# Closing an eight-pass expert stage with tokens on partitions instead of features on partitions

## The reference, cut to what matters

```
def _moe_swiglu(h, w_router, b_router, w_exp_in, w_exp_out):
    logits = (h @ w_router) + b_router
    top_val, top_idx = lax.top_k(logits, 2)
    top_w = jax.nn.softmax(top_val, axis=-1)
    combine = sum(one_hot(top_idx, 8) * top_w[..., None], axis=-2)
    out = zeros_like(h)
    for e in range(8):
        out = out + combine[..., e:e + 1] * _swiglu(h, w_exp_in[e], w_exp_out[e])
    return out

    x = x + gate_f * f              # gate_f: one row of 1024 for the prompt, one for the sample
y = _rmsnorm(x, p["g_final"])       # x * rsqrt(mean(x*x) + 1e-6) * g_final, over the features
```

## Time and profile before

| What | us |
|---|---|
| Median of 3 runs | 1502.15 (1499.78 to 1505.53) |
| Profiled execution, its own time | 1501.98 |
| Span of its profile | 1500.2 |
| PE busy | 1403.1 (94%) |
| DVE busy | 1022.5 (68%) |
| ACT busy | 785.6 (52%) |

### The profile page before, as it was taken

One profiled execution on the slowest core, in us unless ns is written; L12 is line 12 of the kernel. 1 busy time (PEld: TensorE's weight loads), 2 busy tenths in 40 slices (PEclk: granted clock), 3 DMA queues, 4 the chain that ended last, 5 costly groups with the idle time before them and its releaser, 6 DMA issues.

```text
span 1500.2 us, 24401 instructions
## 1 busy us (share of the span) xinstructions
PE 1403.1 (94%) x9312; PEld 1234.5 (82%) x9312; DVE 1022.5 (68%) x1417; ACT 785.6 (52%) x1062; POOL 38.2 (3%) x66
## 2 busy tenths in 40 slices
PE   5899999998889999998999999988899999999984
PEld 4788999875889999996989988767588888888863
DVE  2376999874554444334769987744788898889855
ACT  2534448634433333225443586243778788778852
POOL 0000100000000000000001000000200000000100
PEclk8999999999989999999999999999899999999996
DMA  9856743124446867434858661245689999999951
GB/s 310 228 169 197 235 141 125 59 85 154 135 140 201 255 217 237 177 100 121 246 159 290 198 186 57 85 140 188 223 320 386 383 387 388 378 386 385 384 203 68
DMA packets 280099, 327.33 MB, mean 218 GB/s; under 512 B 32319, under 2 KB 190471, under 8 KB 280007
## 3 DMA queue, kind: packets, MB, share of 16 engines
q1 hardware_dynamic: 273042, 314.29, 63.0%
q10 hardware_dynamic: 5492, 6.53, 1.3%
q0 software_dynamic: 1472, 5.24, 1.0%
HBM read 310.84 MB, written 15.17 MB: 217 GB/s over the span
## 4 chain that ended last, share of the span: by engine, by line
PE 88%; DVE 5%; ACT 2%; DMA 2%; SPq 1%; issue 1%; ACTq 0%; POOLq 0%; POOL 0%; DVEq 0%
PE mmp L819 14%; PE mmp L821 14%; PE mmp L820 13%; PE mmp L1221 8%; PE mmp L1223 8%; PE mmp L1222 8%; PE mmp L813 7%; PE py L789 2%; PE px L869 2%; PE py L885 1%; PE lg L985 1%; PE lg L869 1%; PE px L1027 1%; DVE hT L1796 1%; DMA ring<-in_w_ada_dram 1%
## 5 line engine op out<-in xcount | busy, mean ns | idle before, releaser
L819 PE MATMUL mmp<-hT_hi,wm_hi 128*128 128x320 f32 (+1 forms) x976 | 308.3, 316 | 13.1 <-DVE merged_lo L2023 5.1
L821 PE MATMUL mmp<-hT_hi,ring_lo 128*128 128x320 f32 (+1 forms) x976 | 306.2, 314 | 0.0
L820 PE MATMUL mmp<-hT_lo,wm_hi 128*128 128x320 f32 (+1 forms) x848 | 263.3, 310 | 0.0
L1827 DVE TENSOR_TENSOR ring_lo<-ring,wm_hi 128x1024 fp32r<-128x1024 f32 (+1 forms) x124 | 148.1, 1201 | 86.5 <-ACT wm_hi L1423 84.3
L819 PEld LDWEIGHTS mmp<-hT_hi,wm_hi 128*128 128x128 f32 (+1 forms) x976 | 184.7, 189 | 18.6 <-issue 8.4
L821 PEld LDWEIGHTS mmp<-hT_hi,ring_lo 128*128 128x128 f32 (+1 forms) x976 | 184.3, 189 | 0.2
L1423 ACT CAST wm_hi<-ring 128x1024 fp32r<-128x1024 f32 (+1 forms) x124 | 126.7, 1029 | 101.5 <-PE mmp L821 80.7
L820 PEld LDWEIGHTS mmp<-hT_lo,wm_hi 128*128 128x128 f32 (+1 forms) x848 | 159.3, 188 | 0.2
L1380 ACT ACTIVATE tmp<-mmp 128x320 f32<-128x320 f32 x70 | 30.7, 438 | 231.5 <-PE mmp L821 163.1
L1915 DVE SCALAR_TENSOR_TENSOR conv<-u_conf,dwc,conv 128x350 f32<-128x350 f32 x240 | 132.2, 581 | 3.1
L2048 DVE TENSOR_TENSOR wd_lo<-ring,wd_hi 128x2048 fp32r<-128x2048 f32 (+1 forms) x34 | 75.7, 2229 | 64.6 <-ACT wd_hi L1587 64.5
(11 more groups left out here) (371 smaller groups left out, 2866.2 us busy)
## 6 DMA issues: line engine op xcount, KB each, us to landing
ring<-in_w_in_dram SPq DMA_DIRECT2D x104, 512.0 KB, 4.6
ring<-in_w_exp_in_dram SPq DMA_DIRECT2D x64, 512.0 KB, 8.2
more<-in_w_exp_in_dram SPq DMA_DIRECT2D x64, 512.0 KB, 11.2
ring<-in_w_ada_dram SPq DMA_DIRECT2D x56, 512.0 KB, 7.2
more<-in_w_exp_out_dram SPq DMA_DIRECT2D x48, 512.0 KB, 6.9
ring<-in_w_ffn_in_dram SPq DMA_DIRECT2D x44, 512.0 KB, 5.9
wide<-in_w_ada_dram SPq DMA_DIRECT2D x40, 512.0 KB, 7.6
ring<-in_w_branch_dram SPq DMA_DIRECT2D x48, 256.0 KB, 2.8
```

The source lines that it names most:

```text
L819: nc.tensor.matmul(out, w_hi, x_hi, start=is_first, stop=False)
L820: nc.tensor.matmul(out, w_hi, x_lo, start=False, stop=False)
L821: return nc.tensor.matmul(out, w_lo, x_hi, start=False, stop=is_last)
L1827: V.tensor_tensor(mix_rows(ring_lo, l, s, r), mix_rows(ring, l, s, r), mix_hi(l, s, r).bitcast(F32), ALU.subtract).then_inc(mix_lo_ready, 1)
```

## The change

The late rows are gathered before the last pass has ended. What they hold of the last pass's rows is stale, and gets weight zero. The last pass's own y is not stored: for each token that has a row in it, a selection matrix `Sz` [128 tokens, 128 rows] holds the token's weight at that row (DVE, L2270 of the new file); PE transposes it to `SzT` (L1286), ACT copies it (L1720). After the last pass DVE multiplies y by the gate, once for the prompt's gate row and once for the sample's. For each third t of the tokens PE then forms, in two banks, `SzT`'s product with that gated y (L1315, 512 columns wide) plus the transposed residual, by products of `xT` with the identity (L1318, eight of 128 columns). DVE adds the other rows (`both_rows`, with gate; `add_z`), and ACT gets the sum of squares of a token along its row. The root and reciprocal are of one number a token. The gate rows and g_final must now lie along the free dimension on every partition: sixteen DMAs in the mixer of layer 1 store the gate by 4-byte elements to `gate_dram`, and SP loads it back broadcast behind the last weights. SP issues the outputs.

```diff
@@ SP, layer 1, gates
                         if l:
                             clear_rows(j)
+                        if l and j == 8:
+                            sp.wait_ge(mods_added, DEPTH * ADA_PAIRS)
+                            for s_ in range(2):
+                                for c in range(DC):
+                                    sp.dma_start(gate_dram[s_, c * P:(c + 1) * P].unsqueeze(1),
+                                                 mods[:, l, 40 + c, s_:s_ + 1]).then_inc(gate_stored, 16)
@@ SP, behind the last pass's loads
+                    sp.wait_ge(xg_done, last + 1)
+                    sp.wait_ge(gate_stored, 16 * 2 * DC)
+                    sp.dma_start(gate_rows[0][:], gate_dram[0:1, :].broadcast_to([P, D])).then_inc(gate_loaded, 16)
+                    sp.dma_start(gate_rows[1], gate_dram[1:2, :].broadcast_to([P, D])).then_inc(gate_s_loaded, 16)
+                    sp.dma_start(fin_row, g_final.unsqueeze(0).broadcast_to([P, D])).then_inc(fin_loaded, 16)
+                    for t in range(3):
+                        sp.wait_ge(out_ready, t + 1)
...
@@ POOL
                 if c == 1:
-                    pool.wait_ge(y_saved, last * 16 + 16)
-                    nc.gpsimd.sem_inc(y_free, 1)
+                    pool.wait_ge(chunk_done, last * CPP + (ring_no["moe", 1, 0] + 12))
@@ PE, in the last pass, then behind it
+                                    if k == 10 and is_last_pass:
+                                        pe.wait_ge(sz_ready, 1)
+                                        for t in range(3):
+                                            ins = nc.tensor.transpose(lg[:, t * P:t * P + rows[t]], Sz[0:rows[t], t, :],
+                                                                      ident[0:rows[t], 0:rows[t]])
+                                        ins.then_inc(sz_tr, 1)
-                    pe.wait_ge(y_evac, last + 2)
+                    pe.wait_ge(szT_ready, 1)
                     for t in range(3):
-                        pe.wait_ge(rows_summed, t + 1)
-                        for c in range(DC):
-                            ins = nc.tensor.transpose(sum_bank(c)[:, t * P:t * P + rows[t]],
-                                                      y_late[0:rows[t], t, c * P:(c + 1) * P],
-                                                      ident[0:rows[t], 0:rows[t]])
...
-            norm_sums(4)
-            pe.wait_ge(h_ready, DC * 5)
...
+                        for h in range(2):
+                            pe.wait_ge(y_gated_ready, h + 1 if t < 2 else 3)
+                            c = slice(h * 512, (h + 1) * 512)
+                            nc.tensor.matmul(z_banks(t)[0:rows[t], c], SzT[:, t * P:t * P + rows[t]],
+                                             y_gated[t // 2][:, c], start=True, stop=False)
+                            for c in range(4 * h, 4 * h + 4):
+                                ins = nc.tensor.matmul(z_banks(t)[0:rows[t], c * P:(c + 1) * P],
+                                                       xT[:, c, t * P:t * P + rows[t]], ident[:], start=False,
+                                                       stop=(c % 4 == 3))
+                        ins.then_inc(z_done, 1)
@@ ACT, in the last pass, then behind it
+                            if k == 11 and is_last:
+                                act.wait_ge(sz_tr, 1)
+                                copy(SzT[:], lg[:, 0:T]).then_inc(szT_ready, 1)
+                            if k == 15 and is_last:
+                                act.wait_ge(ab_ready, 1)
+                                act.wait_ge(early_rows, 16 * 3)
+                                for t in range(3):
+                                    m = P if t < 2 else TS
+                                    nc.scalar.activation(x_tok[0:m, t, :], x_tok[0:m, t, :], ACT.Copy,
+                                                         scale=w_ab[0:m, 0, t:t + 1]).then_inc(early_scaled, 1)
+                                nc.scalar.activation(root[:, 0, :], eps[:, 0:1], ACT.Sqrt)
-                            if k == CPP - 1:
+                            if k == CPP - 1 and not is_last:
...
+                        act.wait_ge(z_added, t + 1)
+                        nc.scalar.activation(z_banks(t)[0:m, :], y_late[0:m, t, :], ACT.Square,
+                                             accum_out=sum_sq[0:m, t, :]).then_inc(z_squared, 1)
+                        act.wait_ge(z_squared, t + 1)
+                        nc.scalar.activation(root[0:m, t, :], sum_sq[0:m, t, :], ACT.Sqrt, scale=1.0 / D,
+                                             bias=eps[0:m, 0:1]).then_inc(root_ready, 1)
@@ DVE, router, then last pass
+                    link(V.tensor_scalar(row_end, cum[:, NE - 1:NE], NE - 1.0, float(P), ALU.add, ALU.mult))
...
+                    link(V.tensor_scalar(row_z, pos_ab[:, 1, :].unsqueeze(2), row_end, None, ALU.subtract))
+                    link(V.tensor_scalar(in_z, row_z, -0.5, None, ALU.is_gt))
+                    link(V.tensor_tensor(w_z, in_z, w_ab[:, 1, :].unsqueeze(2), ALU.mult))
+                    link(V.tensor_tensor(w_ab[:, 1, :].unsqueeze(2), w_ab[:, 1, :].unsqueeze(2), w_z, ALU.subtract))
...
+                            if k == 5 and is_last:
+                                dve.wait_ge(y_saved, last * 16)
+                                for t in range(3):
+                                    ins = V.tensor_scalar(Sz[:, t, :], iota_f[:], row_z[:, t, :], w_z[:, t, :],
+                                                          ALU.is_equal, ALU.mult)
```

More of the change, by code:

```diff
@@ L319, in build @@
         gap, w_top, w_ab, swap, row_0 = table(3), table(2, 3), table(2, 3), table(2, 3), table(3, 1)
+        row_z, in_z, w_z, row_end = table(3, 1), table(3, 1), table(3, 1), table(1)
+        sum_sq, root, r_root = table(3, 1), table(3, 1), table(3, 1)
+        assert table_at[0] <= 480
+        Sz = y[:, 0:3 * P].rearrange("p (t s) -> p t s", t=3)
+        SzT = std
+        y_gated = (y, hid_tok[:, 0:D])
+        fin_row = more[:, 0, D:2 * D]
+        gate_rows = (xrow, more[:, 1, D:2 * D])
+        gate_dram = nc.dram_tensor("gate_dram", (2, D), F32).ap()
         rlT = std[0:NE, :]
@@ L1259, in run_pass @@
                                 hid_transposes(2)
-                            if k == 16 and not is_last:
+                            if k == 16 and not is_last_pass:
                                 pe.wait_ge(xrow_full, p * 16 + 16)
@@ L2228, in _, with both_rows @@
                     run_pass(last, True)
[L2229 to L2230 removed]
+                    def both_rows(t):
                         m = P if t < 2 else TS
                         dve.wait_ge(early_scaled, t + 1)
[L2233 to L2240 removed]
@@ L2242, in _ @@
-            norm(4)
-            for b in range(6):
-                t, g = b // 2, b % 2
-                m = P if t < 2 else TS
-                dve.wait_ge(y_tr, b + 1)
-                V.tensor_copy(x_tok[0:m, t, g * 512:(g + 1) * 512], mmp[0:m, b % 4, :]).then_inc(y_copied, 1)
+                        link(V.scalar_tensor_tensor(y_late[0:m, t, :], y_late[0:m, t, :], w_ab[0:m, 1, t:t + 1],
+                                                    x_tok[0:m, t, :], ALU.mult, ALU.add))
+                        link(V.tensor_tensor(y_late[0:m, t, :], y_late[0:m, t, :], gate_rows[t // 2][0:m, :], ALU.mult))
@@ new lines, in add_z, with end_row @@
+                    def add_z(t):
+                        m = P if t < 2 else TS
+                        dve.wait_ge(z_done, t + 1)
+                        V.tensor_tensor(y_late[0:m, t, :], z_banks(t)[0:m, :], y_late[0:m, t, :],
+                                        ALU.add).then_inc(z_added, 1)
+                    def end_row(t):
+                        m = P if t < 2 else TS
+                        dve.wait_ge(root_ready, t + 1)
+                        link(V.reciprocal(r_root[0:m, t, :], root[0:m, t, :]))
+                        V.scalar_tensor_tensor(x_tok[0:m, t, :], y_late[0:m, t, :], r_root[0:m, t, :], fin_row[0:m, :],
+                                               ALU.mult, ALU.mult).then_inc(out_ready, 1)
@@ new lines, in _ @@
+                    dve.wait_ge(late_rows, 16 * 3)
+                    dve.wait_ge(gate_loaded, 16)
+                    for t in range(2):
+                        both_rows(t)
+                    dve.wait_ge(chunk_done, last * CPP + (n0 + CPP))
+                    dve.wait_ge(gate_s_loaded, 16)
+                    for h in range(2):
+                        c = slice(h * 512, (h + 1) * 512)
+                        V.tensor_tensor(y_gated[0][:, c], mmp[:, 2 + h, :], gate_rows[0][:, c],
+                                        ALU.mult).then_inc(y_gated_ready, 1)
@@ L2251 @@
+                    V.tensor_tensor(y_gated[1], mmp[:, 2:4, :].rearrange("p a b -> p (a b)"), gate_rows[1],
+                                    ALU.mult).then_inc(y_gated_ready, 1)
+                    both_rows(2)
```

(7 more changed lines are left out.)

68 lines of the change are left out of this document (26 added, 42 removed).

## The result

The changed kernel takes 1491.78 us (median of 5 runs, 1489.74 to 1493.42) where the kernel before takes 1502.15 (1499.78 to 1505.53): ratio 0.9927, 95% interval 0.9911 to 0.9944. In a later comparison on another occasion it was 1489.53 against 1503.26, ratio 0.9911 [0.9896, 0.9927]. The gain is 10 to 14 us; I had forecast 23.5 and a time of 1478.6.

What follows compares the result with a forecast made beforehand. The end was taken as bound by latency: 44.6 us in series after the last matmul. Replacing them by 21.2 gains 23.4, ending at 1476.8; with 1.8 us of execution beyond the span, 1478.6, range 1475 to 1487.

Steps and rivals of the forecast that it cites:

- the 21.3 that my sum has behind the last matmul's start: Tail: the new series of DVE, PE, ACT and output DMA takes 21.2 us from the last matmul's end, replacing 44.6.
- the arrival of the late rows: End of the last pass: late gather asked for near 1440, landed between 1449.2 and 1451.9, DVE starting at 1451.3.
- The gate stores: Layer 1's mixer: sixteen stores in SP's queue delay the j=9 load 1.2 us, with some 20 us to spare; cost nothing.
- The 7.3 us for the packets' time: Gate stores in layer 1's mixer: 2048 packets at 57 ns each over 16 engines take 7.3 us, hidden.
- Rival C: Layer 1's mixer: gate stores run serially; at 4.2 us each the stall is 39.7 us, time 1518; chance 3%.
- the bound of 1454: Behind the last pass: latest start of DVE's `both_rows` on the late rows, taken at 1451.3 with bounds 1450.6 and 1454.
- rival B: End of the last pass: late rows or gate row come after 1454, or last weights are delayed; 1481 to 1484.5; 10%.
- rival A: PE's pause after the last pass: clock falls to half speed, losing 2.8 to 3.3 us: 1482, worst near 1489.5; 15%.
- DVE's own four operations: Behind the last pass: DVE's operations for two thirds of the late rows take 5.2 us with links, until 1456.5.
- A third of PE's products: Tail: two 512-column selection products and eight identity products take 3.6 us at the full clock, 7.2 at half.
- rival D: End: something else, such as output DMAs or ACT-DVE hand-overs at twice the price, gives 1483 to 1484; 9%.
- DVE's small router operations and the selection: Router and passes: five tiny operations 1.0 us, three selection operations in waits; costed nothing, at most 1 us each.

Runs made afterwards that it cites:

- b_stores: The kernel before with the sixteen gate stores alone added in SP's queue at the same place: 1502.47 us, ratio 1.0002.
- a_spread: The changed kernel with one gate store behind each of the sixteen branch and out loads of layer 1: 1492.75 us, ratio 0.9937.
- b_small480: The kernel before with table `small` 480 columns wide instead of 448, later tiles 128 bytes further on: six passes 288.36 us for 286.79 (one execution).
- a_best2: The changed kernel with gates transposed and stored by two DMAs, `small` at 448, late broadcasts, PE's operands first, one DVE wait moved: 1478.43 us, ratio 0.9840.
- b_small512: The kernel before with table `small` 512 columns wide, later tiles 256 bytes further on: six passes 286.79 us, as before (one execution).
- a_bcast_late: The changed kernel with the sample's gate row and g_final broadcasts asked for later, at the last pass's chunk before the last: 1487.42 us (one execution).
- a_filler: The changed kernel with six unused identity products on PE right behind the last pass: first bank 1.82 us for 3.43, tail 24.06 (one execution).
- a_flat_stores: The changed kernel with each gate store replaced by one of 128 adjacent zeros, 16 packets for 2048: 1486.59 us, ratio 0.9908.
- a_reorder: The changed kernel with DVE making PE's gated operands after only the first both_rows, the others later: 1483.20 us, ratio 0.9860.
- a_pool_stores: The changed kernel with the sixteen gate stores issued from POOL's own queue, earlier, instead of SP's: 1493.08 us, ratio 0.9948.

## Why the prediction was wrong

The forecast of 1478.6 was 14.8 us below the first profiled run of the changed kernel, 1493.42. By the table these are: start of the span 2.7 (noise), mixer 3.9, router -0.4, first pass 2.8, six passes 1.6, last pass 0.5 more than my 0.33, tail 3.7 more than the 21.3 that my sum has behind the last matmul's start.

Only part of it repeats. The second profile, 5.9 us above the forecast, has 4.1 in the tail, 1.6 in the six passes, 0.5 in the last one, 3.0 in the first, nothing in the mixer, the router 0.6 shorter and a start 2.6 earlier. So the step that failed in both, and by most, is the arrival of the late rows with the pause and the clock behind it. The stores, costed at nothing, are 2.6 us in the mean of seven profiles. The place of the tiles was no term of the sum, and the first pass stays open.

**The gate stores were costed at nothing.** I had the load of j=9 leave 1.2 us late, land in 5 us and have some 20 us to spare. All three were wrong in the changed kernel. First, SP's issues were not 0.55 us each as in the earlier trace rows, they were 0.72 (11.58 for sixteen), and the load left 4.0 us late. Second, it took 12.5 us to land for 5.4: in 884 to 892 us DMA was 0.63 to 0.66 busy at 31 to 53 GB/s, where before 876 to 888 ran at 152 to 241.

```profile
884.00:888.00 4.00, 4.00 (x31) 3.31 (x30) 3.68 (x8) 3.97 (x7) 0.00 (x0) 1.00 0.63 31
888.00:892.00 4.00, 4.00 (x29) 4.00 (x29) 3.69 (x6) 3.04 (x8) 0.00 (x0) 1.00 0.66 53
892.00:896.00 4.00, 4.00 (x33) 3.48 (x31) 1.35 (x3) 1.07 (x3) 0.00 (x0) 1.00 1.05 364
```

Third, I read the spare time from PE, 20 us until it takes up the chunk. The chunk is read first by ACT's cast and DVE's subtraction. Before the change the load had landed at 881.1 and ACT cast the chunk at 889.35, 8.2 us later. The 4.0 and the 7.1 us used that up and left the 2.9 that ACT waited (the chunk's cast before, then in the changed kernel):

```profile
889.35 1.04 ACT L1423 CAST wm_hi<-ring 128x1024 fp32r<-128x1024 f32 x1
```

```profile
895.08 1.04 ACT L1456 CAST wm_hi<-ring 128x1024 fp32r<-128x1024 f32 x1 [2.93 <-DMA ring<-in_w_in_dram]
```

The 7.3 us for the packets' time look nearly right, since q1's packets took 63.5% of b_stores's span, 954.3 us, for 63.0% or 945.1 before. That is luck. In the trace's record of single packets a 4-byte one takes 9 ns and not my 57, about 1.3 us in all over 16 engines. The time went into the weights' own 1 KB packets: in 884 to 892 us of the changed kernel most of them took 46 ns as ever, but a few up to 4.2 us, 253 ns in the mean, where before 876 to 888 has 56. Rival C had the right place and the right sign of the effect, with a wrong mechanism: the stores are not serial at 4.2 us, they slow what shares the engines with them. The page of the Trainium skill that I weighed and set aside, "DMA: Bandwidth & Descriptors" (section "Specifications"), says that a transfer below 512 B becomes a read-modify-write. I had taken that as double time for the small packets; their recorded 9 ns don't show it. In a_spread too the sixteen stores raised the DMA share of 30 us from 0.27 to 0.74 by longer weight packets (124 ns in the mean for 51). Whether a read-modify-write is behind that, no run shows.

**The tiles' place was no step of the sum.** `small` grew by 32 columns, and the prediction read the line as bookkeeping. It costs 1.6 us in six passes, found by b_small480 and taken back in a_best2. In the last pass b_small480 has 58.78 us for 57.98, as much as the changed kernel with its three transposes (0.42 us, 0.33 predicted), but b_small512 has 58.45, so that there the placement is not all.

**The late rows came 2.1 us later than I took them.** They were asked for at 1451.38, against my 1440 plus the 11.4 us by which the pass ends later: as said. DVE took them up at 1464.77 for 1451.3 plus 11.4, which is 1.5 us beyond my upper estimate of their arrival too, though inside the bound of 1454 that I had set for DVE's start. POOL's three issues had 3.2 us between first and last, for 3.65 in the earlier trace rows. But I let them land at 5.3 to 7.9 us and they took 9.4. I had the rows go first and the 1.5 MB of broadcast rows behind them. SP issued the broadcasts 3.7 us before the gather was even asked for, so that they and the last weights were in the engines when it came (share 1.03 to 1.05 until 1460):

```profile
1447.68 0.35 SPq L743 DMA_DIRECT2D xrow<-gate_dram  x1
1448.08 0.42 SPq L744 DMA_DIRECT2D more<-gate_dram  x1
1448.55 0.43 SPq L745 DMA_DIRECT2D more<-in_g_final_dram  x1
```

I had said that "the new 2.8 MB have some 6 us before 1451.3", at 0.80 share; 2.8 MB at the 385 GB/s of the passes alone are 7.3. a_bcast_late took 1 MB away and DVE's wait was gone. This is rival B in cause, below its own condition of 1454, and rival A in consequence, which I had priced apart: with DVE's own four operations (5.2 us, as predicted) PE paused 4 us instead of 1.3, and the clock was at half speed for its first bank, 1.7 us by a_filler. Together the 2.1 and the 1.7 us are about the tail's 3.7. My figure for A was 2.8 to 3.3; two variants come to it, a_flat_stores and a_spread, where the clock was at 0.50 before PE's first product and PE's products to the end took 21.8 us instead of 19.0. a_reorder cut the pause to 1.75 us and kept the full clock, with late rows that came no earlier.

**What was right.** A third of PE's products is 3.5 us at the full clock, predicted 3.6 (0.86 to 0.92 a product); `both_rows`, the gated halves, `add_z`, the square with its root (1.5 us) and the last DMA's 3.3 us are all within 0.3 of their terms; rival D did not occur. DVE's small router operations and the selection were hidden as far as the stretches show. In a_best2, with the causes removed, the gain is the 23.5 us of the forecast, which is partly luck: its tail is 19.7 for my 21.3, and it has a better order on DVE that the forecast didn't know.

**What stays open.** Why the first pass begins at the lower clock in some executions of either kernel (0 to 3 us; the mean of C-D is 37.7 for the kernel before and the five built on it, 38.3 for the eleven of the changed one); why SP needs 8.8 us for the sixteen stores in one execution and 11.0 to 12.2 in the others; what makes the weights' packets long; and what decides the clock behind a short pause. The first column of the table differs by up to 5 us between executions, so that a pair of profiles settles a small term only where its stretch is cut out, as the six passes were.

## What to carry to other kernels

Spare time for a transfer ends where its first reader waits, the cast and not the matmul; and new transfers are to be added up in bytes against what the engines have left in that stretch, together with everything else that the change asks for there. Columns of single 4-byte elements should not leave a core while weights stream: turn them on PE first and store rows. When a tile grows, look at what lies behind it: keep later tiles where they were, or compare the repeated stage of the loop before and after.

## What the runs showed of the hardware

- Sixteen DMAs of 128 elements of 4 bytes cost 0 to 4.6 us of stall in a stream of 512 KB loads, thirty-two 14.3, and sixteen spread over a quieter stage 7. From POOL's queue, at an earlier place, they cost 8.2. A 4-byte packet itself was recorded with 9 ns; a 512 KB load behind the sixteen stores landed in 11.7 to 12.7 us for 5.4.
- Moving SBUF tiles by 128 bytes made the median matmul record of L1221, with DMA and two other engines beside it, 393 ns instead of 389, and a pass 48.06 us instead of 47.80, the same to 0.01 us in every execution; moving them by 256 bytes cost nothing in the six passes.
- PE's pauses of 0.88, 1.75, 1.97 and 2.37 us behind a pass at the full clock were followed by the full clock, those of 2.85, 3.64, 3.95, 3.96 and 4.35 us by half the clock. But one of 3.12 us (a_pool_stores) was followed by the full clock as well: the length of the pause alone does not decide it. The half clock cost 1.7 us in three of the five and 2.8 in the other two.
